# Ten RMS norms with the sum of squares per token on partitions, the root taken on 128x2, and PE spreading the reciprocal

## The reference

```python
def rms_norm(x, g):
    xf = x.astype(jnp.float32)
    y = xf * lax.rsqrt(jnp.mean(xf * xf, axis=-1, keepdims=True) + EPS)
    return (y * g.astype(jnp.float32)).astype(x.dtype)

def modulate(h, shift, scale):
    return h * (1 + scale) + shift
```

## Time and profile before

| | us |
|---|---|
| median of 3 runs | 2050.88 (2050.53 to 2053.23) |
| profiled execution, its own time | 2045.0 |
| its span | 2043.2 |
| PE busy in it | 1702.8 (83%) |
| DVE busy | 573.0 (28%) |
| ACT busy | 417.5 (20%) |

### The profile page before, as it was taken

One profiled execution on the slowest core, in us unless ns is written; L12 is line 12 of the kernel. 1 busy time (PEld: TensorE's weight loads), 2 busy tenths in 40 slices (PEclk: granted clock), 3 DMA queues, 4 the chain that ended last, 5 costly groups with the idle time before them and its releaser, 6 DMA issues.

```text
span 2043.2 us, 22615 instructions
## 1 busy us (share of the span) xinstructions
PE 1702.8 (83%) x9278; PEld 1089.1 (53%) x9278; DVE 573.0 (28%) x1302; ACT 417.5 (20%) x732; POOL 18.5 (1%) x26
## 2 busy tenths in 40 slices
PE   6899989999999999996888777677687967766776
PEld 4544357887888886553744333343345624333433
DVE  3242145117888536546230000000024000000002
ACT  4222241002220023212221111111123211111111
POOL 0000000000110000000000000000000000000000
PEclk9999897999999999887868988888897878888888
DMA  9425730244558835105659999999985899999994
GB/s 365 174 78 206 292 124 1 83 165 173 201 182 329 309 111 202 41 6 202 250 236 402 429 427 429 427 430 427 425 317 214 337 429 428 429 428 430 427 430 199
DMA packets 110595, 571.81 MB, mean 280 GB/s; under 512 B 9121, under 2 KB 15393, under 8 KB 85954
## 3 DMA queue, kind: packets, MB, share of 16 engines
q1 hardware_dynamic: 109488, 568.66, 69.2%
q10 hardware_dynamic: 1042, 2.24, 0.3%
HBM read 569.83 MB, written 1.05 MB: 279 GB/s over the span
## 4 chain that ended last, share of the span: by engine, by line
PE 60%; DMA 30%; DVE 5%; ACT 2%; issue 2%; SPq 1%; DVEq 0%; ACTq 0%
DMA ring<-in_w_exp_up_dram 29%; PE bank L461 19%; PE bank L1105 10%; PE bank L805 8%; PE bank L832 4%; PE bank L469 3%; PE bank L487 2%; PE bank L848 1%; PE bank L1182 1%; PE bank L541 1%; PE bank L512 1%; PE bank L1124 1%; PE bank L1133 1%; PE bank L1091 1%; DMA ring<-in_w_ada_dram 1%
## 5 line engine op out<-in xcount | busy, mean ns | idle before, releaser
L1105 PE MATMUL bank<-ring,arena 128*32 128x512 f32 x1952 | 296.3, 755 | 217.0 <-DMA ring<-in_w_exp_up_dram 215.1
L1105 PEld LDWEIGHTS bank<-ring,arena 128*32 128x32 f32 x1952 | 80.6, 134 | 425.0 <-issue 422.3
L2350 DVE TENSOR_TENSOR arena<-arena,bank 128x256 f32<-128x256 f32 x32 | 13.5, 422 | 622.0 <-ACT arena L1630 622.0
L461 PE MATMUL bank<-ring,hT 128*128 128x512 f32 (+4 forms) x480 | 161.0, 492 | 6.5 <-issue 4.9
L805 PE MATMUL bank<-hT,ring 128*128 128x256 f32 x704 | 156.2, 384 | 4.2 <-ACT hT L1336 4.2
L805 PEld LDWEIGHTS bank<-hT,ring 128*128 128x128 f32 x704 | 135.2, 193 | 23.2 <-issue 4.6
L1124 PE MATMUL bank<-ring,arena 128*32 128x512 f32 x1024 | 129.2, 650 | 1.9 <-DVE arena L2350 1.9
L461 PEld LDWEIGHTS bank<-ring,hT 128*128 128x128 f32 x480 | 86.8, 192 | 75.8 <-issue 66.3
L1626 ACT COPY arena<-bank 128x512 f32<-128x512 f32 x32 | 33.5, 1046 | 444.8 <-PE bank L1105 444.8
L1133 PE MATMUL bank<-arena 128*128 (+1 forms) x512 | 119.1, 386 | 1.6 <-DVE arena L2354 1.6
L1133 PEld LDWEIGHTS bank<-arena 128*128 128x128 f32 x512 | 94.6, 190 | 41.1 <-issue 26.0
(11 more groups left out here) (311 smaller groups left out, 1718.6 us busy)
## 6 DMA issues: line engine op xcount, KB each, us to landing
ring<-in_w_exp_down_dram SPq DMA_DIRECT2D x64, 2048.0 KB, 17.6
ring<-in_w_exp_up_dram SPq DMA_DIRECT2D x62, 2048.0 KB, 23.3
ring<-in_w_exp_gate_dram SPq DMA_DIRECT2D x60, 2048.0 KB, 18.8
ring<-in_w_mod_dram SPq DMA_DIRECT2D x24, 2048.0 KB, 13.4
ring<-in_w_ada_dram SPq DMA_DIRECT2D x12, 2048.0 KB, 13.7
ring<-in_w_up_dram SPq DMA_DIRECT2D x10, 2048.0 KB, 11.4
ring<-in_w_in_dram SPq DMA_DIRECT2D x8, 2048.0 KB, 14.1
ring<-in_w_down_dram SPq DMA_DIRECT2D x5, 2048.0 KB, 9.3
```

Of the source, the lines that this page charges most:

```text
L461: ins = pe.matmul(b, lhs(k), rhs(k), start=(k == 0), stop=(k == n - 1))
L1105: ins = pe.matmul(bank[0][32 * q:32 * q + 32, :], xe[:, k * CAP:(k + 1) * CAP], xs[q // 2][:, o:o + 512], start=(k == 0), stop=(k == KD - ...
```

## The change

The sums of squares come out with tokens on partitions: the block of squares (128 features x 128 tokens) becomes the stationary operand, and two columns of ones the moving one. Per block there are two products with two output columns each, in place of one with 256 columns. The bank then holds two useful columns, one per 128 tokens. ACT's root reads them into a small tile root_col (128x2, two alternating), DVE inverts 128x2, and PE transposes each column, broadcast to 128x128, back into the same bank (spread_root), so that every partition again has all 256 values. DVE's multiplications read them from PSUM, and only when all eight are done does DVE count the bank as read.

```diff
             def norm_part(c, b, lo, hi):
                 for k in range(lo, hi):
                     pe.wait_ge(sem("squares"), KD * c + k + 1)
-                    ins = pe.matmul(b[:, 0:T], ones, (sq_late if c in (7, 9) else sq)[:, k, :], start=(k == 0), stop=(k == KD - 1))
+                    for tb in range(TB):
+                        ins = pe.matmul(b[:, 2 * tb:2 * tb + 2], (sq_late if c in (7, 9) else sq)[:, k, tb * 128:tb * 128 + 128], ones[:, 0:2],
+                                        start=(k + tb == 0), stop=(k == KD - 1), skip_group_check=True)
                 if hi == KD:
                     G.close(ins, ("ms", c))
+            def spread_root(c):
+                b = bank[G.bank[("ms", c)]]
+                pe.wait_ge(sem("rooted"), c + 1)
+                for tb in range(TB):
+                    ins = pe.transpose(b[:, tb * 128:tb * 128 + 128], root_col[:, 2 * (c % 2) + tb:2 * (c % 2) + tb + 1].to_broadcast(
+                        [128, 128]), ident)
+                G.close(ins, ("rs", c))
+                G.bank[("rs", c)], G.use[("rs", c)] = G.bank[("ms", c)], G.use[("ms", c)]
...
             mod_turn()
+            spread_root(0)
+            spread_root(1)
...
                     if 4 * g + j == CTX_NORM:
-                        norm(3)
+                        norm(3, second=True)
+                    if 4 * g + j == CTX_NORM + 2:
+                        spread_root(3)
...
             norm(4)
+            spread_root(4)
...
                 token_major("ekv", xkv, 256, tb, second=True)
+                if tb == 2:
+                    spread_root(5)
...
             norm(7)
+            spread_root(7)
...
             norm(9)
+            spread_root(9)
...
             def root(c, then=None):
                 b = G.take(act, ("ms", c))
-                if c:
-                    act.wait_ge(sem("scaled"), KD * c)
-                G.give(act.activation(rs, b[:, 0:T], ACT.Sqrt, bias=eps, scale=1.0 / D), ("ms", c))
+                act.activation(root_col[:, 2 * (c % 2):2 * (c % 2) + 2], b[:, 0:4].rearrange("p (t r) -> p t r", r=2)[:, :, 0],
+                               ACT.Sqrt, bias=eps, scale=1.0 / D).then_inc(sem("square_root"), 1)
...
             def invert(c):
-                G.read(dve, ("ms", c))
-                link(dve.reciprocal(rs, rs))
+                r = root_col[:, 2 * (c % 2):2 * (c % 2) + 2]
+                dve.wait_ge(sem("square_root"), c + 1)
+                dve.reciprocal(r, r).then_inc(sem("rooted"), 1)
 
             def norm(c, src, g, dst):
-                if c:
-                    invert(c)
+                rs = G.take(dve, ("rs", c))[:, 0:T]
                 for k in range(KD):
-                    dve.scalar_tensor_tensor(dst[:, k, :], src[:, k, :], g[:, k:k + 1], rs,
-                                             ALU.mult, ALU.mult).then_inc(sem("scaled"), 1)
+                    ins = dve.scalar_tensor_tensor(dst[:, k, :], src[:, k, :], g[:, k:k + 1], rs, ALU.mult, ALU.mult)
+                    ins.then_inc(sem("scaled"), 1)
+                dve.wait_ge(sem("scaled"), KD * (c + 1))
+                dve.sem_inc(freed[G.bank[("rs", c)]], 1)
```

More of the change, by code:

```diff
@@ L272, in build @@
         gain = sb("gain", [128, 8 * KD])
-        rs = sb("rs", [128, T])
         xT = sb("xT", [128, KD, T])
@@ L402, in build @@
         nul = small[:, 2:4]
+        root_col = sb("root_col", [128, 4])
         m_gt = gsm[:, 0:64].rearrange("p (b c) -> p b c", b=4)
@@ L525, in outputs_and_norm @@
                 norm_part(c, b, KD - 3, KD)
+                spread_root(c)
             def normed(c, k=KD):
@@ L1362, in _ @@
                 mod(i)
+            root(1)
             shift(0, mc(0, 0), hT[:, :, 0:T])
-            root(1)
             shift(1, mc(0, 0, 1), hT[:, :, T:2 * T])
@@ L1499, in _ @@
                     act.activation(gel[:, (j - 1) % 3, :], gel[:, (j - 1) % 3, :], ACT.Gelu).then_inc(sem("gelu_done"), 1)
-                if j == CTX_NORM + 2:
+                if j == CTX_NORM + 4:
                     shift(3, mc(1, 0, 1), hT[:, :, T:2 * T])
@@ L1766, in _ @@
                 mod(i)
+            invert(1)
             set_gain(0, mc(0, 1), vc("norm1_g", 0, KD))
@@ L1967, in _ @@
                 G.read(dve, ("wo", n))
+            invert(2)
             norm(2, xT, gains(2), hT[:, :, 0:T])
@@ L1984, in _ @@
                 if j == CTX_NORM:
+                    invert(3)
+                if j == CTX_NORM + 2:
                     set_gain(4, mc(1, 1, 1), vc("g_norm1_2", 0, KD))
@@ L2006, in _ @@
             dve.wait_ge(sem("ff_added"), KD)
+            invert(4)
             norm(4, xT, vc("final_g", 0, KD), xT)
@@ L2012, in _ @@
             evict(("ekv", 2), e_kv[:, 2, :], 256)
+            invert(5)
             norm(5, xT, gains(3), hT[:, :, 0:T])
@@ L2283, in experts @@
                 set_gain(c - 1 - layer, mc(1 + layer, 4), vc("g_norm2_2", KD * layer, KD))
+                invert(c)
                 norm(c, xT, gains(c - 1 - layer), hT[:, :, 0:T])
@@ L2365, in _ @@
             link(dve.tensor_tensor(gains(0), mc(2, 2), vc("s_pool_2", 0, KD), ALU.mult))
+            invert(7)
             norm(7, xT, gains(6), hT[:, :, 0:T])
@@ L2372, in _ @@
             experts(1, 8)
+            invert(9)
             norm(9, xT, vc("g_final_2", 0, KD), xT)
```

## The result

The changed kernel takes 2063.48 us (median of 4 runs, 2061.47 to 2063.80) against 2050.70 of the kernel before in the same session (4 runs, 2050.17 to 2053.23): 1.0058 of it, interval 1.0040 to 1.0075. It is slower, as forecast, but by 12.8 us instead of 6.1, and outside the range. A second session with more runs gives 2062.99 against 2050.78, 1.0068 (1.0054 to 1.0083).

A forecast was written before the change was run, and what follows sets the result against it. PE, and from 1092.5 us on the experts' transfers, were taken to set the pace. Norm terms +0.9, clock falls +4.8 and weaker run-up +0.4 made +6.1 on the median 2050.88: 2057.0 us, range 2050.5 to 2061.

The forecast's parts named there:

- up to norm 2: Norm 0: the reciprocal now runs on DVE ahead of its gains, +0.15 us.
- norm 3, and the product behind it: Norm 3: transposes add 0.45 us to PE's stream and the sums save 0.3, +0.15; no clock fall.
- norm 4: wait for the bank: Norm 4: the keys' first product waits for DVE's eight multiplications to free the sums' bank, +3.9 us.
- norm 5: Norm 5: PE stops within ekv for DVE's eviction, reciprocal and the transposes, 1.2 us less 0.3 for sums, +0.9.
- norm 6; norm 8: Norms 6 and 8: the shorter path saves 1.05 us and the sums 0.3, -1.35 each; Exp's table costs nothing yet.
- norm 7: sums and wait: Norm 7: the pooling product waits for all of DVE's multiplications, losing its overlap, +0.95 us.
- norm 9: Norm 9: path -1.05 us, sums -0.3, multiplications from PSUM +0.1, together -1.25.
- The path of root, reciprocal and spreading: From root to first multiplication: 1.33 us instead of 2.40, saving 1.05, with four transpose records at 0.63.
- The sums save nothing: Sums of squares on PE: 32 two-column records take 3.15 us against 3.47 for 16 wide ones, 0.3 saved.
- The clock: Behind norms 4 and 7: PE's clock falls where two-column sums and a wait lie together, 2.4 us each, +4.8.
- Rival (b): Norms 4 and 7: the waits come but the clock holds in one or both; 2052.2 to 2054.6 us, chance 0.22.
- Rival (e): Transposes at half clock in norms 4, 6, 7, 8, 9, no gain in sums, larger falls; 2062 us, chance 0.07.

The follow-up runs named there:

- wide_sums: The changed kernel with 128 equal columns of sums in place of two, records, waits and banks unchanged; 2056.56 us, ratio 1.0031.
- fill2: The kernel before with 16 more unread products (32 records) of two columns ahead of norm 3's sums; 2053.58 us.
- fill128: The kernel before with 16 more unread products (32 records) of 128 columns ahead of norm 3's sums; 2052.12 us.
- fill2_long: The kernel before with 32 unread products (64 records) of two columns ahead of norm 3's sums; 2064.83 us.
- fill128_long: The kernel before with 32 unread products (64 records) of 128 columns ahead of norm 3's sums; 2058.84 us.
- both: The changed kernel with 128 columns in the sums and the spread values in a bank of their own; 2045.56 us, ratio 0.9980.
- own_bank: The changed kernel, two-column sums kept, with the spread values in a bank of their own, so the root frees the sums' bank; 2059.96 us, ratio 1.0052.
- both_n5: The kernel both with norm 5's reciprocal moved ahead of an eviction on DVE; 2045.70 us, ratio 0.9976.
- tuned: The kernel both with the spreading of norms 4 and 5 put behind products that need not wait for it; 2048.15 us, ratio 0.9990.

## Why the prediction came out where it did

The stage terms measured are shifts of the changed trace against that of before. The accounting is that of two profiled executions, 2061.47 and 2045.0, 16.5 us apart, where the medians are 12.8 apart.

| step | forecast, us | measured, us |
|---|---|---|
| up to norm 2 | +0.15 | +4.8 |
| norm 2 | -1.2 | -1.06 |
| norm 3, and the product behind it | +0.15 | +2.0 |
| norm 4: wait for the bank | +3.9 | +4.1 |
| norm 4: keys at a lower clock | +2.4 | +2.7 |
| norm 5 | +0.9 | +4.6 |
| norm 6; norm 8 | -1.35 each | -1.26; -1.28 |
| norm 7: sums and wait | +0.95 | +2.3 |
| norm 7: pooling product | +2.4 | +1.6 |
| logits of norms 6 and 8 | +0.4 | +0.1 |
| norm 9 | -1.25 | -0.1 |

- **The path of root, reciprocal and spreading** came out at 1.34 us against 1.33 in norm 2, but by luck. Root 0.27 and reciprocal 0.18 are as the rows said. The forecast had four records of transposes at full clock, 0.63. The spreading is two records, and in norms 2, 4, 7 and 9 they ran at a granted clock of 0.50 and took 0.70. At 1.00 the two take 0.43 (norms 5, 6 and 8). There the path is 1.05 (norm 6, 1025.42 to 1026.47), below the 1.3 to 1.4 that the prediction named as its sign.
- **The bank of norm 4** was right, with DVE's last multiplication ahead of the keys: 4.1 against 3.9.
- **The sums save nothing**: this term (0.3 in norms 3 to 9, 0.15 in norm 2) was mis-sized. 32 records take 3.47 us at full clock, as much as the 16 wide ones. I went by L501's eight records in 0.79 us, too few to read a rate from: four records of the new sums show as 0.34 us and 32 as 3.47, so that each further record costs 0.112, and a short group looks cheaper than it is. The Trainium skill, page "TensorE: Matmul & The Clock Gate", section "LDWEIGHTS (loading the stationary operand)", was the better guide here: by the 107 ns a record estimated from it the sums would take 3.4 us, and the trace has 108.
- **The clock** is the step that failed. The prediction put falls only where the sums and a wait lie together, in norms 4 and 7 (+4.8), and nothing in norms 3, 5 and 9. The sums alone lost it there, with PE busy throughout: norm 3 (8.70 instead of 6.91), norm 5 (0.9 in the sums and 2.55 in ekv), norm 9 (sums 4.50 instead of 3.47, which takes back nearly all that was to be won). That is 6.3 us without a term. wide_sums, which keeps every wait, brings all of them back to full speed (6.91; 3.57 and 3.47; 3.58).
- **Norms 4 and 7** got about the size that was forecast (2.7 and 1.6, and 0.95 in norm 7's sums, against 2.4 each), but not by the forecast's course of events. The clock fell within the sums, not in the wait behind them, and the wait then kept it down. The prediction had itself noted for the logits of norms 6 and 8 that products of few columns did not hold the clock, and did not carry that over to sums with no wait behind them.
- **Norms 6 and 8** came out within 0.1, again by errors that cancel: the sums saved 0.05 instead of 0.3 (1.69 against 1.74), and from root to logits 1.22 went instead of 1.05. Exp's table (1.28 us from 1025.70 on in norm 6) did become the last long step ahead of the logits, as forecast.
- **Up to norm 2** is mostly a matter of which execution was profiled. fill2, fill128 and their long forms are word for word the kernel before up to norm 3, and reach one product behind the attention (L461) at 438.18, 437.30, 442.32 and 441.19, where the profile of before had it at 433.73. The profile of before, 2045.0, was at the low end of its own runs (2044.5 to 2054.3). At startup the changed kernel does lose clock: its two groups of sums take 3.66 and 3.74 us, and behind each 16 records of L487 take 3.26 and 3.21, where such a group takes 1.92 in the kernel before. It reaches the mixer's first product at 43.40 instead of 41.67, but the four kernels with fillers reach it at 41.98 to 45.75, so no run tells how much of the 1.7 is the change's.
- Two readings of the earlier trace rows were a little off, without a consequence: in norm 6 the clock fell 0.95 us after the logits began, not over a microsecond, and its rise in norm 8's transposes was at 1556.8.

From norm 2 on the terms add up to +13.7, and the stretches between take back 2.0 (0.6 in the product behind norm 2, 1.0 between the second keys and the product at 976.59 of before, 1.0 in the second layer's experts, with +0.6 in small pieces): 11.7, the same in the repeat's trace. The forecast had +5.95 for this part (6.1 less startup's 0.15), so 5.7 too little. Norms 3, 5 and 9 alone, 6.5 us measured against -0.2, are more than that, and wide_sums shows their cause. The medians are 12.8 and 12.2 apart; what of the 0.5 to 1.1 us on top lies before 438 us stays open.

Rival (b) supposed that two-column products might count for the clock, which fill2_long against fill128_long speaks against. Rival (e) came nearest in time, 2062. Two of its three parts did happen, transposes at half clock (in norms 4, 7 and 9) and no gain in the sums; but it too had no fall in norms 3, 5 and 9, and transposes at half clock added next to nothing to the forecast's price for them (0.70 against 0.63).

What stays open: where exactly the clock falls in a run of narrow products, and when it does not. The same 32 records lost it in norm 3 of the changed kernel and held it in fill2.

## What to carry to other kernels

Before narrowing a product on PE, look at its weight loads: with 128 weights to load for each one, 2 columns took nearly as long as 128 (3.47 and 3.57 us for 32 records), and the run of narrow ones cost PE its clock for the products behind it in most places. Count the records of a small product in a trace of the same form before pricing it, and look at the granted clock under it. When the reader of a PSUM bank changes, follow who gives that bank back and which next product opens it; and try such repairs together, since here each alone gave 3 and 7 us of a loss of 12 and both together 17. The form to use in this kernel is `both`: sums of 128 columns and a bank of its own for the spread root, 0.9980 of the kernel before (0.9971 to 0.9989). Some of that may be luck: at the second keys and behind them it kept the clock where the kernel before itself lost 1.7 us in other traces (fill128 and fill128_long, the same program there).

## What the runs showed of the hardware

- The granted clock fell from 1.00 to 0.50 while PE was busy 2.00 of 2.00 us in every row (fill2_long, from 578 us on), with no empty stretch ahead, and stayed at 1.00 in the twin with 128 columns. In these two traces PE's busy share in the profile was the same, the granted clock was not.
- In norm 4 of the changed kernel the clock fell at 726.4 us, as 3.48 us of two-column sums ended; with 128 columns (wide_sums) it fell at 731.4, 4.5 us behind the sums (2.2 in the repeat); with 128 columns and no long wait (both) it stayed at 1.00.
- Two records of 128x128 transposes took 0.70 us at a granted clock of 0.50 and 0.43 at 1.00 (L523, norms 4 and 6 of the changed kernel).
- The kernel before varies between 2044.5 and 2054.3 us with nothing changed. Up to norm 3 the same program reached one product at 433.7 us in one profile and at 437.3 to 442.3 in four others.
- The runs of 16-column egt products, the same in all kernels, lost the clock in some profiles and not in others. One stands ahead of the second keys: 64 records of keys behind it took 13.91 us in the kernel before, the changed kernel, own_bank and both, 15.60 in wide_sums and fill128_long, 16.44 in both_n5 and 16.84 in tuned. The other begins the 160 records of L461 behind those keys: they took 38.03 in the kernel before, wide_sums and both, 39.71 in the changed kernel, own_bank and fill128, and 41.37 in tuned.
